# PEER expert stage on one NeuronCore: six query projections ahead of the experts, and the sixth head's weights loaded into the accumulator's memory

## The reference, cut to what matters

```python
def peer_block(hblk):                      # D_MODEL 2048, 8 heads, top 16
    q  = (hblk @ w_q).reshape(..., PEER_HEADS, 2, 128)
    s1, s2 = q[..., 0, :] . k1, q[..., 1, :] . k2      # 128 scores each
    v1, i1 = top_k(s1, 16);  v2, i2 = top_k(s2, 16)
    score, pos = top_k(v1[:, None] + v2[None, :], 16)  # of 256 sums
    idx  = (i1 * 128 + i2)[pos];  gate = softmax(score)
    act  = gelu(w_u[idx] . hblk)                       # 16 dot products of 2048
    return sum_k gate * act * w_v[idx]                 # 16 rows of 2048
```

## Time and profile before

| | us |
|---|---|
| median of three runs | 3030.87 |
| profiled execution, its own time | 3028.67 |
| its span in the profile | 3027.0 |
| output projection, from the load of x to its last product | 1577 to 1663 |
| first query projection begins | 1675 |
| first gather issued | 1702 |
| last product of the experts | 3021 |
| PE busy over the span | 2623.6 (87%) |
| DVE busy | 1959.7 (65%) |
| GpSimd busy | 612.5 (20%) |

### The profile page before, as it was taken

How to read it: one execution, slowest core, us unless ns; L and a number is a source line. 1 busy time by engine, 2 the same in 40 slices (tenths; PEclk the granted TensorE clock), 3 DMA queues, 4 the chain that set the end, 5 groups by cost and what they waited for, 6 DMA issues and landing times.

```text
span 3027.0 us, 31557 instructions
## 1 busy us (share of the span) xinstructions
PE 2623.6 (87%) x11033; PEld 1796.4 (59%) x11033; DVE 1959.7 (65%) x2660; ACT 960.6 (32%) x1298; POOL 612.5 (20%) x580
## 2 busy tenths in 40 slices
PE   7999988999989999999999867869688776768777
PEld 3578766878767889998877723334344333323322
DVE  4689996444666778887545775655556555656656
ACT  5567775433554433333433210101011111101100
POOL 0000000000000000000000374334353434443333
PEclk9999998999999999999999988989999898989999
DMA  8733334543324868887555799999999999999999
GB/s 341 271 118 111 125 110 142 192 154 108 129 84 177 359 264 343 337 331 285 206 211 209 296 419 412 422 411 421 421 410 421 403 421 409 421 400 421 421 422 374
DMA packets 126513, 902.91 MB, mean 298 GB/s; under 512 B 14016, under 2 KB 15552, under 8 KB 17216
## 3 DMA queue, kind: packets, MB, share of 16 engines
q0 software_dynamic: 82944, 604.02, 48.4%
q1 hardware_dynamic: 38736, 278.94, 24.5%
q10 hardware_dynamic: 4720, 18.57, 1.6%
HBM read 899.33 MB, written 2.13 MB: 298 GB/s over the span
## 4 chain that ended last, share of the span: by engine, by line
PE 41%; DMA 31%; DVE 12%; issue 10%; ACT 3%; POOL 2%; DVEq 0%; ACTq 0%; POOLq 0%; SPq 0%
DMA u<-in_peer_u,idx 28%; PE ps L457 10%; PE ps L500 8%; PE ps L502 8%; PE ps L501 8%; PE ps L807 4%; DVE u L1805 2%; DMA v<-in_peer_v,idx 2%; DVE wl L1231 2%; DMA w<-in_stream 1%; POOL v L1900 1%; ACT wh L904 1%; PE ps L513 1%; PE ps L472 1%; DVE ub L1367 1%
## 5 line engine op out<-in xcount | busy, mean ns | idle before, releaser
L807 PE MATMUL ps<-v,dg 128*128 128x512 f32 x1920 | 878.0, 613 | 176.6 <-DMA v<-in_peer_v,idx 101.6
L1805 DVE SCALAR_TENSOR_TENSOR u<-u,hN 128x2048 f32<-128x2048 f32 x256 | 586.5, 2292 | 472.0 <-DMA u<-in_peer_u,idx 460.7
L1231 DVE TENSOR_TENSOR wl<-w,wh 128x1024 fp32r<-128x1024 f32 x432 | 524.6, 1222 | 408.3 <-ACT wh L904 407.8
L807 PEld LDWEIGHTS ps<-v,dg 128*128 128x128 f32 x1920 | 368.0, 196 | 682.5 <-issue 510.7
L904 ACT ACTIVATE wh<-w 128x1024 fp32r<-128x1024 f32 x432 | 453.5, 1058 | 606.9 <-PE ps L502 411.2
L1890 POOL DMA_INDIRECT u<-in_peer_u,idx x256 | 286.5, 1119 | 844.3 <-DVE u L1805 453.9
L457 PE MATMUL ps<-both,wh 128*128 128x256 f32 x2048 | 372.3, 285 | 5.3 <-DVE y L1495 5.1
L1182 ACT ACTIVATE dg<-con,wt 128x128 f32<-128x128 f32 x240 | 93.3, 400 | 841.3 <-PE ps L807 836.3
L457 PEld LDWEIGHTS ps<-both,wh 128*128 128x128 f32 x2048 | 320.9, 193 | 10.2 <-issue 9.0
L1900 POOL DMA_INDIRECT v<-in_peer_v,idx x256 | 291.7, 1139 | 172.8 <-PE ps L807 87.0
L1882 POOL DMA_DIRECT2D mr<-in_wmod x64 | 34.0, 532 | 1371.2 <-DVE br_lo L1623 953.2
(11 more groups left out here) (254 smaller groups left out, 2884.1 us busy)
## 6 DMA issues: line engine op xcount, KB each, us to landing
w<-in_stream SPq DMA_DIRECT2D x260, 1024.0 KB, 4.8
mr<-in_wmod POOLq DMA_DIRECT2D x64, 1024.0 KB, 7.1
wg<-in_gates ACTq DMA_DIRECT2D x8, 512.0 KB, 3.4
wx<-in_stream SPq DMA_DIRECT2D x4, 1024.0 KB, 7.9
u<-in_peer_u,idx POOLq DMA_INDIRECT x256, 16.7
v<-in_peer_v,idx POOLq DMA_INDIRECT x256, 18.0
xs<-in_ctx ACTq DMA_DIRECT2D x1, 2048.0 KB, 7.7
xs<-in_x ACTq DMA_DIRECT2D x1, 2048.0 KB, 14.4
```

Of the source, the lines that this page charges most:

```text
L807: last = mm(ps[:, b, :], dg[:, k % 4, :], V[n % NV][:, b * 512:(b + 1) * 512], start=(k == 0), stop=(k == TOPK - 1))
L1231: tt(wl[p % SPLITS][:, :, :], W[s][:, q * PIECE:(q + 1) * PIECE, :], wh[p % SPLITS][:, :, :].bitcast(F32), ALU.subtract)\
L1805: stt(U[n % NU][:, :], U[n % NU][:, :], 1.0, hN[:, t, :], ALU.mult, ALU.mult, accum_out=dot[:, t, k:k + 1])\
```

## The change

Weights of head 5 get a place of their own, WA, in the memory of `acc`, which is cleared later for that reason, after head 0's first dot products and after `route(5)`. They are loaded by ACT's queue at the head of the output projection, ahead of x. PE makes the queries of heads 4 and 5 before the experts begin, and the two remaining ones (heads 6 and 7) in the turns of heads 0 and 1, behind `scores` instead of ahead of it. Heads 4 and up take PSUM banks 4 and 7 in turn.

```diff
+        WA = [sb(f"wa{s}", R_HX + 16384 + 8192 * NU + s * HB, [P, HK, CW]) for s in range(2)]
+        wa_in = [sem(f"wa_in{s}") for s in range(2)]
...
+        def query_bank(h):
+            return h if h < 4 else (4, 7)[h % 2]
...
# SyncE
-            for h in range(4, PH):
+            for h, of in ((4, 0), (6, 4), (7, 6)):
                 for s in (0, 1):
-                    sp.wait_ge(piece_used, 2 * (WQ0 + 2 * (h - 1 if h > 4 else 0) + s + 1))
+                    sp.wait_ge(piece_used, 2 * (WQ0 + 2 * of + s + 1))
                     sp.dma_start(W[s][:, :, :], a_stream[WQ0 + 2 * h + s].rearrange("p (k n) -> p k n", n=CW)).then_inc(arrived[s], 16)
...
# TensorE, route(h)
+                    elif h == 5:
+                        w, in_, n = WA[q], wa_in[q], 16
                     else:
-                        w, in_, n = W[q], arrived[q], 16 * (WQ0 // RING + h - 2)
+                        w, in_, n = W[q], arrived[q], 16 * (WQ0 // RING + {4: 2, 6: 3, 7: 4}[h])
                     pe.wait_ge(in_, n)
-                    if h > 4 and q == 0:
-                        pe.wait_ge(*AR.at(h - 1, "q"))
+                    if h > 5 and q == 0:
+                        pe.wait_ge(*AR.at(h - 2, "q"))
...
-                            last = mm(ps[:, min(h, 4), blk * T:(blk + 1) * T], w[:, kk, blk * P:(blk + 1) * P], hT[:, k, :],
+                            last = mm(ps[:, query_bank(h), blk * T:(blk + 1) * T], w[:, kk, blk * P:(blk + 1) * P], hT[:, k, :],
...
# TensorE, the order
             route(3)
+            route(4)
+            route(5)
             pe.wait_ge(*AR.at(3, "q"))
             for h in range(PH):
                 experts(h, 0)
-                if h + 4 < PH:
-                    route(h + 4)
                 if h + 2 < PH:
                     scores(h + 2)
+                if h + 6 < PH:
+                    route(h + 6)
                 if h + 1 < PH:
                     experts(h, 1)
...
# ScalarE, head of the output projection
             act.wait_ge(piece_used, 2 * WO0)
+            for s in range(2):
+                act.dma_start(WA[s][:, :, :], a_stream[WQ0 + 10 + s].rearrange("p (k n) -> p k n", n=CW)).then_inc(wa_in[s], 16)
             act.dma_start(x2[:, :, :], a_x.rearrange("(t p) d -> p t d", p=P)).then_inc(x2_in, 16)
...
# ScalarE, queries(h)
-                fn(qT[:, h % 3, :, :], ps[:, min(h, 4), :].rearrange("p (s t) -> p s t", s=2), ACT.Copy).then_inc(*AR.inc("q"))
+                fn(qT[:, h % 3, :, :], ps[:, query_bank(h), :].rearrange("p (s t) -> p s t", s=2), ACT.Copy).then_inc(*AR.inc("q"))
...
# VectorE, output projection
                     low(WO0, i, 16, 20)
-                    nc.vector.memset(acc[:, :, :], 0.0).then_inc(*VF.inc("acc0"))
                     dve.wait_ge(rows_in, 48)
...
# VectorE, experts
             dots(0, 0, second)
+            dve.wait_ge(piece_used, 2 * (WQ0 + 12))
+            nc.vector.memset(acc[:, :, :], 0.0).then_inc(*VF.inc("acc0"))
             dots(0, 1, route(1, 0, 1, False))
```

More of the change, by code:

```diff
@@ L347, in build @@
         VW = Steps(sem("dve_wout"), [f"{w}{c}{t}" for c in (0, 1) for t in (0, 1) for w in ("m", "a")], primed=True)
-        VF = Steps(sem("dve_ffn"), ["acc0", "g1", "ss", "rc", "x10", "x11"] + [f"hT{k}" for k in range(0, KT, 2)] + ["hm0", "ha0", "hm1", "ha1"])
+        VF = Steps(sem("dve_ffn"), ["g1", "ss", "rc", "x10", "x11"] + [f"hT{k}" for k in range(0, KT, 2)] + ["hm0", "ha0", "hm1", "ha1", "acc0"])
         AF = Steps(sem("act_ffn"), [f"sq{c}{t}" for c in range(NW) for t in (0, 1)] + ["rt", "x00", "x01"] + [f"hT{k}" for k in range(1, KT, 2)])
```

## The result

The changed kernel takes 3049.61 us in the median of four runs (3046.76 to 3050.57), the kernel before 3030.88 us (3029.08 to 3032.56). The ratio is 1.0062 with a 95% interval of 1.0047 to 1.0077: slower by 18.7 us. The profiled execution took 3046.76 us, 18.1 us more than that of before; its span is 3044.9 us, 17.9 us longer.

The account below looks back on a forecast made before the run. The prediction took the expert stage to be bound by its DMA bytes and dry times. Terms -5.0 (bytes), +26.6 (routes behind scores) and -0.5 (hole) sum to +21.1 us, giving 3052.0 us, range 3039 to 3062.

Parts of the forecast that it names:

- hole in the output projection: Output projection: moving the clearing out removes a gap of about 0.5 us between TensorE's products, -0.5 us.
- Bound by bytes: Expert stage: it ends when its bytes are through; each 1.05 MB costs 2.49 us, two halves fewer give -5.0 us.
- Routes 4 and 5 at no cost: Before the experts: two more routes, 28.0 us, fit TensorE's idle 27.85 us, cost 0.
- Routes 6 and 7: Turns 0 and 1: routes behind the scores block GpSimd 14.0 us longer and dry the DMA engines, +26.6 us with turn 2.
- the cushion is already used up: Each turn: queued gathers have run out when TensorE returns to the experts, so each further microsecond of stop is uncovered.
- The clock: Behind the scores: some 2.4 us at half speed cost 1.2 us, paid by the route instead of the experts, net 0.
- Clearing acc: Expert stage, about 1765 us: VectorE's 3.47 us of clearing meet idle time and queued gathers; bounds 0 and +3.5, taken 0.
- WA ahead of x: Output projection: 2.1 MB more ahead of x, landing after about 15 to 17 us; bounds 0 and +5.0, taken 0.
- A: Rival, turns 0 and 1: the queue of gathers absorbs the later start, not slower, 3025.4 us; chance 7%.
- B: Rival, turns 0 and 1: some 11 us of the two 14.0 are got back, about 3041 us; chance 10%.
- C: Rival, output projection: WA slows weights or x, or the clearing holds up GpSimd, +5, 3057.0 us; chance 12%.
- D: Rival: the routes behind the scores stay at 1.2 GHz, 28 us each, +28 more, 3080 us; chance 2%.

Follow-up runs that it names:

- e1: The changed kernel with the routes of heads 6 and 7 ahead of the scores again: 3028.43 us, ratio 0.9996.
- e3: The changed kernel with routes ahead of scores again and acc cleared later, behind late dot products of head 0's tile 1: 3025.45 us, ratio 0.9985.
- e7: e3 without the two loads of head 6's weights, head 6 using head 4's weights instead: 3020.2 us, ratio 0.9963.
- d16: The kernel before with 16 more products behind the scores of turns 4 and 5: 3038.87 us, one run.
- d64: The kernel before with 64 more products behind the scores of turns 4 and 5: 3081.54 us, one run.
- after_again: The changed kernel, unaltered, measured once more: 3048.11 us, ratio 1.0060.
- e4: The kernel before with only the clearing of acc moved, from the output projection to late dot products of head 0's tile 1: 3029.43 us, ratio 1.0001.
- e5: e3 with VectorE's top-k begun behind dot product 0, so the step the scores wait for comes one dot product earlier: 3022.44 us, ratio 0.9971.
- e6: The kernel before with only VectorE's top-k begun earlier, behind dot product 0: 3026.27 us, ratio 0.9988.

## Why the prediction was right, and which terms were mis-sized

Forecast 3052.0 us, measured 3049.6, within the range of 3039 to 3062 and on the side that had 0.90. The mechanism is shown: e1 moves nothing but the route and takes away all of the loss, with GpSimd's longest wait for V going from 26.1 to 12.4 us. That the number came so near is in part luck: two terms were wrong in size, in opposite directions.

The sum of +21.1, grouped by what the runs can tell apart, and the ratios:

| term | forecast | measured | from |
|---|---|---|---|
| routes behind the scores | +23.0 | +20.0 | after against e1 |
| dips of turns 0 to 2 grow to 3.1 each | +3.6 | | |
| bytes: two halves fewer | -5.0 | | |
| hole in the output projection | -0.5 | | |
| these three together | -1.9 | -4.5 | e3 against before |
| clearing acc in the expert stage | 0 | +3.3 | e1 against e3 |
| sum | +21.1 | +18.8 | |

Each measured entry is a difference of two ratios and good to 3 to 5 us; they add up to the whole because they are neighbouring steps from before to after, which is no test of its own. By stretches of the trace the forecast was: start of the queries -0.5, opening +5.0, turn 0 +10.3, turn 1 +10.2, turn 2 -3.9. Measured were -1.0, +8.8, +8.0, +7.3 and -4.9. The opening's 8.8 are head 6's loads (6.2 by e7) and the clearing (3.3 by the openings) within a microsecond.

Point by point:

- *Bound by bytes, 2.49 us for each 1.05 MB.* Held. Turn 2, which lost head 7's loads and a route that lay within a wait, is 4.9 us shorter, and the opening is 6.2 us shorter without head 6's loads (e7). The prediction weighed the Trainium skill's 358 GB/s ("DMA: Bandwidth & Descriptors", Bandwidth) against 420. The trace of after has 421 in its undisturbed slices. The same section says that its own measurements, up to 425 GB/s, are of one core with the other of its pair idle; that is the case here, and the prediction should have read on to it.
- *Routes 4 and 5 at no cost.* Held: they end at 1760.1, the first products wait 6.38 us more for `dg`. The experts begin at 1766.4, later than the 1761.3 of before, as foreseen (about 1765). It is head 6's loads: counted from the first query product they begin after 86.0 us before, 92.2 after, and 85.8 in e7.
- *Routes 6 and 7.* The right place and sign, but each stop was priced at 3.1 + 14.0 = 17.1 us against a natural dip of some 2, 15.2 more. The mis-sized term is the 3.1, with the step behind it, "the cushion is already used up". The missing GB/s of 15 us windows overstate the dry time: by the landings a turn without loads falls behind by 0.8 to 1.1 us (turns 3 to 5 of the kernel before), and by d16 to d64 some 2 us of a longer stop are still taken up. Against that, the stop was a little longer than 14.0: GpSimd issues its `v` 49.1 us after the end of `experts(1, 0)` and in e1 34.3 us after it, 14.8 later. Less 2 that is 12.8; turn 1 measured 13.1.
- *The clock.* Held within a microsecond. The route pays 1.96 and 1.73 us over 13.98, in after_again 1.21 and 1.10, and the experts behind it get back 56.19 - 55.10 = 1.1; the prediction said 1.2 in either place. So at most some 0.9 us for each turn were missed. The windows of the kernel after show both levels, after an idle time of 27 us:

```profile
1865.00:1870.00 5.00, 3.99 (x14) 3.57 (x15) 2.90 (x6) 0.00 (x0) 0.00 (x0) 0.50 1.01 419
1870.00:1875.00 5.00, 5.00 (x21) 4.25 (x20) 2.67 (x4) 0.00 (x0) 0.00 (x0) 0.82 1.01 416
```

- *Turn 2.* -4.9 against a forecast of -5.0 + 1.1 = -3.9, a microsecond that one pair of runs can't settle. The dip was not going to grow to 3.1: by the landings the turns without loads have 0.8 to 1.1 us in the kernel before.
- *Clearing acc.* The wrong choice between right bounds. "The engines are saturated here" was the reason for 0, but GpSimd was waiting for exactly the buffer that VectorE's next step frees, with the DMA engines at 362 GB/s behind it against 413 with the late clearing.
- *WA ahead of x.* Held, as the projection's length says under e4. x took 13.9 us instead of 7.4, forecast 15 to 17 (rows of the DMA issues, kernel after: count, KB, us to landing), and was needed at 1598.1, 21 us after its issue at 1576.8:

```profile
wa<-in_stream ACTq DMA_DIRECT2D x2, 1024.0 KB, 5.9
x<-in_x ACTq DMA_DIRECT2D x1, 2048.0 KB, 13.9
...
1598.13 0.68 DVE L1720 TENSOR_TENSOR xm<-ps,m2r 128x512 f32<-128x512 f32 x1
```

- *The rivals.* A falls by d16. B had a part of the truth: some 2 us of each stop are got back, not 11 of the two, and at the stop itself, not in the following turn. C's load half falls; its other half, a clearing that holds up GpSimd, is there in the expert stage. D falls: 15.9 us, not 28.

The forecast came nearer than its terms: the dips and stops were some 6 us too dear and the clearing 3 us too cheap.

## What to carry to other kernels

In a stage that is bound by its bytes, ask of each engine that frees buffers how long it may stop before the queue of issued transfers is empty; what goes beyond is paid in full, however idle that engine is on average. Work that needs nothing new goes ahead of the wait it can hide under, never behind it: here that order alone is worth 20 us, and together with the clearing put where its engine has slack it turns the added weight buffer from a loss into the 0.15% that e3 gains. And measure a dry stretch by the gaps between landings, not by GB/s of a short window, which here showed twice the loss that the landings show.

## What the runs showed of the hardware that was not expected

- Windows of 15 us with 313 to 371 GB/s do not mean that the stage loses the missing share. In e5 landings stay 2.5 us apart across a window of 344 GB/s. Several gathers are under way at once (each lands 17 to 18 us after its issue when the queue is full, some seven steps of 2.49), so a short thinning of the queue shows in the rate but is made up before a gather lands. How it is made up is argued, not shown; the size is shown by e5 and e6, which gain 4.2 and 3.6 us where the windows promised 12 and more.
- The same gather that needs 17 to 18 us in the full queue lands 5.6 us after its issue in the empty one (turn 1 of the kernel after).
- Even with the queue full a few landings come some 3.5 us apart instead of 2.49; in e3 those at 2265.3 and 2348.6 us did (the one at 2050.2 us is the first `u` behind a stop, with the queue not yet full). In e5 there are fourteen of them after 1900 us, and each follows 1.5 to 3.3 us, mostly 2.1, behind a packet of 8 KB of queue q14, which the profile calls "instruction". For the landing at 2425.2 us the view of the DMA queues from 2422 to 2426 us has it beside the gathers:

```profile
q0 software_dynamic: 223, 1.68, 101.5%
q14 instruction: 1, 0.01, 0.5%
```

Not every such packet has a late landing behind it (there are 35 in that time), in the kernel after one of six such landings has no packet of q14 near it, and nothing was run to test it: the cause stays open.
